# Two-layer hybrid decoder step on one core: expert residual kept by token, last norm on rows, and three small moves in the mixers

## The reference, cut to what matters

```
h = layer_norm(x)
for i in range(2):
    z = h @ w_in[i]                                   # columns of four token mixers
    a_conv = causal_depthwise_conv(past_a, glu(z_a), conv_a_w[i])           # 31 taps, 256 channels
    y_a = silu(layer_norm(a_conv + conv_a_b[i]))
    ...                                               # gated chunk mixer, short conv, pooling
    h = layer_norm(ALPHA * h + concat(y_a, y_b, y_c, y_d) @ w_out[i])
    f = dense_swiglu(h) if i == 0 else moe_swiglu(h)  # top 2 of 8 experts, gates from a softmax
    h = layer_norm(ALPHA * h + f)
```

## Time and profile before

| what | value |
|---|---|
| runs (three) | 1518.63, 1525.19, 1525.61 us; median 1525.19 |
| the profiled execution's own time | 1527.83 us |
| its span, first to last instruction | 1526.1 us |
| mean granted PE clock | 0.992 |
| busy: PE, DVE, ACT, POOL | 1491.5, 1233.2, 962.4, 91.3 us |
| mixer of layer 0; of layer 1 | about 25 to 115 us; 405 to 503 us |
| dense feed-forward | about 117 to 400 us |
| expert stage, from its first cut | about 532 to 1502 us |
| scatter of the last item and last norm | 1502 to 1526 us |

### The profile page before, as it was taken

The page is one execution under the profiler, slowest core; times in us unless marked ns, Lnnn a source line. Parts: engine busy times, 40 slices in busy tenths (PEclk is TensorE's granted clock), DMA queues, the critical chain, the costliest instruction groups (busy, mean ns, idle before and its releaser), DMA issues.

```text
span 1526.1 us, 20555 instructions
## 1 busy us (share of the span) xinstructions
PE 1491.5 (98%) x7963; PEld 1291.2 (85%) x7963; DVE 1233.2 (81%) x1267; ACT 962.4 (63%) x902; POOL 91.3 (6%) x102
## 2 busy tenths in 40 slices
PE   9999999999998999999999999999999998999997
PEld 8969999999996788888888888888888886878886
DVE  7978555544796698899998988898889897989884
ACT  5645433344564477777777777777777776767773
POOL 3402000000020000001000001000000101100000
PEclk9999999999999999999999999999999999999999
DMA  9725544444250389999999999999999999998980
GB/s 342 156 83 197 177 163 164 166 166 166 88 151 20 146 337 389 376 387 391 405 372 369 376 383 372 404 376 367 379 380 383 399 369 347 364 356 339 370 311 31
DMA packets 68154, 439.43 MB, mean 288 GB/s; under 512 B 9504, under 2 KB 13536, under 8 KB 16608
## 3 DMA queue, kind: packets, MB, share of 16 engines
q1 hardware_dynamic: 60320, 424.68, 73.5%
q0 software_dynamic: 4816, 12.32, 2.7%
q10 hardware_dynamic: 2928, 1.18, 0.3%
HBM read 431.06 MB, written 7.09 MB: 287 GB/s over the span
## 4 chain that ended last, share of the span: by engine, by line
PE 75%; issue 15%; DVE 5%; DMA 3%; ACT 2%; POOL 1%; SPq 0%; ACTq 0%; POOLq 0%; DVEq 0%
PE bank L876 45%; PE bank L550 21%; PE bank L684 2%; PE bank L931 1%; DMA ring<-in_w_e_gate 1%; DVE work L1544 1%; DVE w_lo L1950 1%; PE bank L574 1%; DMA x_rows<-token_rows,token_row 1%; PE bank L529 1%; DVE w_lo L1333 1%; PE bank L496 1%; DMA token_rows<-y_rows 1%; PE bank L512 1%; ACT w_hi L1060 1%
## 5 line engine op out<-in xcount | busy, mean ns | idle before, releaser
L1950 DVE TENSOR_TENSOR w_lo<-ring,w_hi 128x2048 fp32r<-128x2048 f32 x320 | 731.4, 2290 | 96.1 <-ACT w_hi L1261 93.7
L1261 ACT ACTIVATE w_hi<-ring 128x2048 fp32r<-128x2048 f32 x320 | 612.9, 1917 | 162.3 <-PE bank L876 162.2
L876 PE MATMUL bank<-w_hi,x_hi 128*128 128x512 f32 x896 | 353.9, 395 | 0.7 <-DVE w_lo L1950 0.6
L876 PE MATMUL bank<-w_hi,x_lo 128*128 128x512 f32 x896 | 349.3, 390 | 0.0
L876 PE MATMUL bank<-w_lo,x_hi 128*128 128x512 f32 x896 | 348.6, 389 | 0.0
L550 PE MATMUL bank<-x_hi,w_hi 128*128 128x290 f32 x664 | 199.3, 300 | 0.6 <-DVE w_lo L1333 0.5
L876 PEld LDWEIGHTS bank<-w_hi,x_lo 128*128 128x128 f32 x896 | 168.2, 188 | 35.8
L876 PEld LDWEIGHTS bank<-w_hi,x_hi 128*128 128x128 f32 x896 | 168.3, 188 | 35.3 <-DVE w_lo L1950 1.2
L550 PE MATMUL bank<-x_lo,w_hi 128*128 128x290 f32 x664 | 197.6, 298 | 0.0
L550 PE MATMUL bank<-x_hi,w_lo 128*128 128x290 f32 x664 | 197.1, 297 | 0.0
L876 PEld LDWEIGHTS bank<-w_lo,x_hi 128*128 128x128 f32 x896 | 168.4, 188 | 33.3
(11 more groups left out here) (296 smaller groups left out, 1777.1 us busy)
## 6 DMA issues: line engine op xcount, KB each, us to landing
ring<-in_w_e_gate SPq DMA_DIRECT2D x112, 1024.0 KB, 7.1
ring<-in_w_e_up SPq DMA_DIRECT2D x112, 1024.0 KB, 7.3
ring<-in_w_e_down SPq DMA_DIRECT2D x112, 1024.0 KB, 7.4
ring<-in_w_in SPq DMA_DIRECT2D x16, 1024.0 KB, 5.8
ring<-in_w_ff_gate SPq DMA_DIRECT2D x14, 1024.0 KB, 5.2
ring<-in_w_ff_up SPq DMA_DIRECT2D x14, 1024.0 KB, 4.9
ring<-in_w_ff_down SPq DMA_DIRECT2D x14, 1024.0 KB, 4.9
ring<-in_w_out SPq DMA_DIRECT2D x8, 1024.0 KB, 9.7
```

Of the source, the lines that this page charges most:

```text
L876: ins = mm(out, x, w[slot][:, columns], start=(first and n == 0), stop=(last and n == 2), skip_group_check=True)
L1261: A(w_hi[(CUT0 + p) % SPLIT][:, :], ring[(START + p) % SLOTS][:, :], ACT.Copy).then_inc(hi_done, 1)
L1950: V.tensor_tensor(w_lo[(CUT0 + p) % SPLIT][:, :], ring[(START + p) % SLOTS][:, :], w_hi[(CUT0 + p) % SPLIT][:, :].bitcast(F32), ALU.subtra ...
```

## The change

Mixers: (1) ACT makes `sample_prods(16, TAPS_A)` before the two cuts `c1` and `c1 + 1`; (2) the bias rides on tap 0's product on ACT, so that DVE's two additions go; (3) PE runs `keep_warm(7, 20)` ahead of the first sums of norm "a".

Expert stage: (4) the residual is `r_tok`, by token (three tiles of 128 x 1024), started as ALPHA times the input rows, and started only when they stand in `x_rows`; POOL waits for that before it overwrites `x_rows`; (5) `scale_first`, `turn_mix` and `add_mix` are gone; `mix(n)` adds one gathered row times its gate straight to `r_tok`, six DVE operations after chunks 13, 15, 18, 21, 29, 31; (6) the last item's scatter gives rows (tokens by 512 values, six outputs), and DVE adds each with an operation that also sums over the row; (7) the last norm is taken on rows, tile by tile, and then turned by PE and stored by the same four DMAs. Unused waits on `x_lo_done` and the bank reuse `added` go.

```diff
-        SCATTER_BANKS = [6, 7, 1, 4, 5, 2, 3, 6]
+        SCATTER_BANKS = [6, 7, 1, 4, 5, 2]
+        SCATTERED = [(0, 0), (1, 0), (0, 1), (1, 1), (2, 0), (2, 1)]
-        SCALE_AT = [8, 14, 26]
-        MIX_AT = [11, 18, 29]
-        ADD_AT = [17, 21, 27, 33, 39, 41]
-        TURN_AT = [("up", 2), ("gate", 3), ("gate", 4), ("gate", 5), ("gate", 6), ("up", 6)]
+        MIX_AT = [13, 15, 18, 21, 29, 31]
...
@@ PE, mixer
                     if n == 4:
+                        keep_warm(7, 20)
                         next(ln_a)
...
@@ PE, last item
-                for d in range(KB):
...
-                        mm(out, y_hi[q][:, d, :], scat[q][:, :], start=(q == of[0]), stop=False)
-                        last = mm(out, y_lo[q][:, d, :], scat[q][:, :], start=False, stop=(q == of[-1]))
+                for n, (t, half) in enumerate(SCATTERED):
...
+                    out = bank[SCATTER_BANKS[n]][0:rows, :]
+                    for q in range(2):
+                        to = scat[q][:, t * P:t * P + rows]
+                        mm(out, to, y_hi[q][:, 4 * half:4 * half + 4, :], start=(q == 0), stop=False)
+                        last = mm(out, to, y_lo[q][:, 4 * half:4 * half + 4, :], start=False, stop=(q == 1))
                     last.then_inc(scattered, 1)
...
@@ PE, end
-            for _ in ln_sums("ffn1", r, sq_l, lambda b: pe.wait_ge(added, n_items * KB + b + 1)):
-                pass
+            keep_warm(0, 20)
+            for t in range(TT):
+                rows = TILE_ROWS[t]
+                pe.wait_ge(tok_normed, t + 1)
+                for k in range(KB):
+                    last = nc.tensor.transpose(bank[k][:, t * P:t * P + rows], r_tok[0:rows, t, k * P:(k + 1) * P],
+                                               ident[0:rows, 0:rows])
+                    if t == TT - 1:
+                        last.then_inc(y_turned, 1)
...
@@ ACT, sample_prods
+                            if tap == 0:
+                                ins = A(out, src, ACT.Identity, scale=w, bias=v_at("conv_a_b", layer, b))
+                            else:
+                                ins = A(out, src, ACT.Copy, scale=w)
...
@@ ACT, mixer
                 first_taps_c()
+                sample_prods(16, TAPS_A)
                 if layer == 0:
                     act.wait_ge(z_ready, 16)
                     bias_parts(vec_at("ln_mix_b", 0))
                 cut(c1)
                 cut(c1 + 1)
-                sample_prods(16, TAPS_A)
...
@@ ACT, item
-                        if after == "hold" and not tabled and p in SCALE_AT:
-                            scale_first(SCALE_AT.index(p))
...
@@ ACT, end
-            large_ln("ffn1", r, vec_at("ln_ffn_g", 1), vec_at("ln_ffn_b", 1))
+            for t in range(TT):
+                rows = TILE_ROWS[t]
+                act.wait_ge(less_mean_done, n_items * TT + t + 1)
+                A(ring[t][0:rows, 0:D_MODEL], r_tok[0:rows, t, :], ACT.Square, bias=less_mean[0:rows, t:t + 1],
+                  accum_out=sq_sum[0:rows, t:t + 1]).then_inc(tok_sq, 1)
+            for b in range(0, KB, 2):
+                act.wait_ge(y_turned, b + 1)
+                A(h[:, b, :], bank[b][:, 0:TOKENS], ACT.Identity, scale=v_at("ln_ffn_g", 1, b),
+                  bias=v_at("ln_ffn_b", 1, b)).then_inc(y_even, 1)
...
@@ DVE, sample_sums
-                    for b in range(MB):
-                        dve.wait_ge(summed_s, 2 * MB * layer + b + 1)
-                        V.tensor_scalar(sample_cols(acc_a[:, b, :]), sample_cols(acc_a[:, b, :]),
-                                        v_at("conv_a_b", layer, b), None, ALU.add).then_inc(summed_s, 1)
...
@@ DVE, extra_items
-                for d in range(KB):
-                    V.tensor_scalar(r[:, d, :], h[:, d, :], ALPHA, None, ALU.mult).then_inc(r_start, 1)
+                def start_rows(t):
+                    dve.wait_ge(rows_staged, t + 1)
+                    V.tensor_scalar(r_tok[:, t, :], x_rows[:, t % 2, :], ALPHA, None, ALU.mult).then_inc(r_start, 1)
...
@@ DVE
-            def mix(t):
+            def mix(n):
+                t, c = n // 2, n % 2
...
-                dve.wait_ge(mix_scaled, t + 1)
-                V.scalar_tensor_tensor(out=first[0:rows, :], in0=second[0:rows, :], scalar=col[0:rows, 5, t:t + 1],
-                                       in1=first[0:rows, :], op0=ALU.mult, op1=ALU.add).then_inc(rows_mixed, 1)
+                V.scalar_tensor_tensor(out=r_tok[0:rows, t, :], in0=mix_rows[t][c][0:rows, :],
+                                       scalar=col[0:rows, 4 + c, t:t + 1], in1=r_tok[0:rows, t, :], op0=ALU.mult,
+                                       op1=ALU.add).then_inc(rows_mixed, 1)
-            def add_mix(n):
...
@@ DVE, last item
-                for d in range(KB):
-                    dve.wait_ge(scattered, n_scat * KB + d + 1)
-                    V.tensor_tensor(r[:, d, :], r[:, d, :], bank[SCATTER_BANKS[d]][:, 0:TOKENS],
-                                    ALU.add).then_inc(added, 1)
+                for n, (t, half) in enumerate(SCATTERED):
...
+                    V.memset(carrier[:, n:n + 1], 0.0)
+                    row_half = r_tok[0:rows, t, 512 * half:512 * half + 512]
+                    V.tensor_tensor_reduce(out=row_half, in0=bank[SCATTER_BANKS[n]][0:rows, :], in1=row_half, scale=1.0,
+                                           scalar=0.0, op0=ALU.add, op1=ALU.add,
+                                           accum_out=row_sum[0:rows, 2 * t + half:2 * t + half + 1]).then_inc(added, 1)
+                    if half:
...
+                        V.tensor_tensor_reduce(out=halves[0:rows, t, :], in0=row_sum[0:rows, 2 * t:2 * t + 2],
+                                               in1=minus_half[0:rows, 0:2], scale=2.0 / D_MODEL, scalar=0.0, op0=ALU.mult,
+                                               op1=ALU.add, accum_out=less_mean[0:rows, t:t + 1]).then_inc(less_mean_done, 1)
...
@@ DVE, end
+            for t in range(TT):
+                rows = TILE_ROWS[t]
+                dve.wait_ge(tok_sq, t + 1)
+                V.tensor_scalar(var_tok[0:rows, t:t + 1], sq_sum[0:rows, t:t + 1], 1.0 / D_MODEL, LN_EPS, ALU.mult,
+                                ALU.add).then_inc(tok_var, 1)
+                dve.wait_ge(tok_rstd, t + 1)
+                V.tensor_scalar(r_tok[0:rows, t, :], r_tok[0:rows, t, :], less_mean[0:rows, t:t + 1],
+                                rstd_tok[0:rows, t:t + 1], ALU.add, ALU.mult).then_inc(tok_normed, 1)
+            for b in range(1, KB, 2):
+                dve.wait_ge(y_turned, b + 1)
+                V.tensor_scalar(h[:, b, :], bank[b][:, 0:TOKENS], v_at("ln_ffn_g", 1, b), v_at("ln_ffn_b", 1, b),
+                                ALU.mult, ALU.add).then_inc(y_odd, 1)
...
@@ POOL
+                        if i == 1:
+                            pool.wait_ge(r_start, TT)
...
                         if t == 2:
-                            pool.wait_ge(mix_turned, 2)
+                            pool.wait_ge(rows_mixed, 2)
...
+            for t in range(TT):
+                rows = TILE_ROWS[t]
+                pool.wait_ge(tok_var, t + 1)
+                G.tensor_tensor(rstd_tok[0:rows, t:t + 1], var_tok[0:rows, t:t + 1], minus_half[0:rows, t:t + 1],
+                                ALU.pow).then_inc(tok_rstd, 1)
```

More of the change, by code:

```diff
@@ L520, in ln_sums @@
                 yield
-                if name == "ffn1":
-                    keep_warm(1, 4)
                 if MEAN_BANK[name] == 7:
@@ L531, in ln_sums @@
                 yield
-                if name == "ffn1":
-                    keep_warm(1, 7)
                 pe.wait_ge(ln_rs, n + 1)
@@ L894, in _ @@
                 pe.sem_inc(s, 2 * TABLED)
-            def turn_mix(n):
-                t, half = n // 2, n % 2
-                rows = TILE_ROWS[t]
-                pe.wait_ge(rows_mixed, t + 1)
-                if n:
-                    pe.wait_ge(mix_added, n)
-                for k in range(4):
-                    kk = 4 * half + k
-                    last = nc.tensor.transpose(bank[7][:, k * P:k * P + rows], mix_rows[t][0][0:rows, kk * P:(kk + 1) * P],
-                                               ident[0:rows, 0:rows])
-                last.then_inc(mix_turned, 1)
             def item(i, e, x_from, after, x_next=None, tabled=False):
@@ L965, in item @@
                         number_rows(x_next)
-                    if after == "hold" and not tabled and ("gate", g) in TURN_AT:
-                        turn_mix(TURN_AT.index(("gate", g)))
                     turn(g - 1)
                     hidden("up", g)
-                    if after == "hold" and not tabled and ("up", g) in TURN_AT:
-                        turn_mix(TURN_AT.index(("up", g)))
                     down(g - 1, 0)
@@ L1230, in _ @@
                 act.wait_ge(s, 64 * DEPTH)
-            def scale_first(t):
-                rows = TILE_ROWS[t]
-                first = mix_rows[t][0]
-                act.wait_ge(mix_rows_in[t], 32)
```

(9 more changed lines are left out.)

87 lines of the change are left out of this document (46 added, 41 removed).

## The result

The changed kernel took 1502.19 us (median of 4 runs, 1501.92 to 1503.56); the kernel before, beside it, 1523.03 us (4 runs, 1518.63 to 1525.61). The ratio is 0.9856 with a 95% interval of 0.9834 to 0.9879. Forecast were 1501.1 us and a range of 1493 to 1510.

What follows compares the result with a forecast made beforehand. PE was taken to bound the expert stage, so only work or waits taken off PE pay. Terms 0 - 4.8 - 14.1 - 5.2 = -24.1 us from 1527.8 give 1503.7, less 2.6 for the median 1501.1; range 1493 to 1510.

Steps and rivals of the forecast that it cites:

- Mixer 1: Norm "a" of mixer 1: earlier products, bias edit and ones start the squares' sums at 478.8, against 483.59; -4.8 us.
- Mixer 0: Norm "a" of mixer 0: ones end 1.6 us after the sums' old start, full clock makes up for it; 0.
- The bounds: Both mixers: if the ones did not hold the clock up, mixer 1 wins only 2.2 us and mixer 0 loses 1.7.
- Item 6: Item 6 of the expert stage: two waits and six turns go, less 0.9 us of short PE waits; -14.1 us.
- The two waits: Item 6: waits behind `scale_first(0)` and at `turn_mix(5)` go with their clock losses, 8.4 and 3.7 us.
- The turns: Item 6: six turns, each putting 0.36 to 0.43 us between matmuls, go; 2.5 us.
- DVE as the bound: Rival, item 6: four mixes in nine cuts make PE wait and lose clock, 3.7 us at two places, 1508; chance 0.13.
- Loads that give the stall back: Rival, item 6: busy DMA queues turn the stall into waits on loads; half 1507, all 1510; chance 0.12.
- The end: From the scatter on: scatter in rows, norm tile by tile, last blocks shared by ACT and DVE; -5.2 us.
- The stores behind it are the same: The end: the stores after ACT's last block were taken as unchanged.
- The exit of the loop: The end: if the loop's exit also costs 1.3 us, the end wins only 2.5 us, its low end.
- Normalising 128 x 1024: The end: not in the trace, priced at 0.8 us; 0.59 by the skill's page, with 0.6 us more won.

Runs made afterwards that it cites:

- run 1: The changed kernel without the 20 ones products ahead of the sums of norm "a" in the mixers; 1499.65 us, ratio 0.9829.
- run 4: The kernel before with three places in item 6 moved (first scaling, first mix, fifth addition), its turns and scales kept; 1515.98 us, ratio 0.9921.
- run 6: The kernel before with the mixers' three edits alone (products ahead of the cuts, bias in ACT's first tap, ones products); 1521.70 us, ratio 0.9976.
- run 11: The kernel before with only the products of taps 16 to 30 moved ahead of the two cuts; 1519.66 us (one run).
- run 12: As run 9, with the six mixes of item 6 after chunks 13, 17, 19, 23, 29, 31; 1499.93 us, ratio 0.9828.
- run 10: The changed kernel again, unaltered, on the chip of runs 9, 11 and 12; 1501.97 us, ratio 0.9847.
- run 9: The changed kernel with the edits of runs 1 and 7 together; 1499.53 us, ratio 0.9835.
- run 3: The changed kernel with the products of taps 16 to 30 behind the two cuts again; 1506.37 us, ratio 0.9861.
- run 8: The changed kernel without the 20 ones products behind the scatter at the end; 1502.36 us (one run).
- run 7: The changed kernel with the last norm's variances ahead of the previous tile's normalising and 20 of the end's 40 ones records; 1500.61 us, ratio 0.9839.

## Why the prediction came out right, point by point

- **Mixer 1, forecast -4.8, measured -5.4.** The steps held: the sums start behind the ones at 474.04 (474.8 forecast), then 3.9 us to the squares' sums (4.0). The ones' 4.63 us are the forecast 4.7; PE ended its block 0.5 us earlier. That the cuts cost nothing held: one waits for its chunk as before, and DVE comes to them much later.
- **Mixer 0, forecast 0, measured -0.3.** The trade of ones against clock came out even, as worked out. The bounds ("if the ones did not hold the clock up, mixer 1 would win only 2.2 and mixer 0 lose 1.7") took for granted that without the ones the clock would be down after 3 us. This is a step whose reason fell, beside that of the stores below: in that state it is down in some executions and up in others, and run 1 was faster without the ones.
- **Item 6, forecast -14.1, measured -14.5.** The two waits were priced with their clock losses at 8.4 + 3.7 + 0.4 = 12.5 us; run 4 took 12.2 away by places alone. The turns less PE's new waits were 2.5 - 0.9 = 1.6 in the forecast and 2.3 by subtraction. PE's new short waits came to 0.8 us as two pieces of 0.48 and 0.33, against 0.9 forecast. That the forecast agrees this well is partly luck: the stall of 6.08 us was one execution's, and in runs 6 and 11 it was 3.5 and 2.8 us shorter, the expert stage 4.1 and 3.2 us.
- **DVE as the bound** got only those 0.8 us; run 12 shows that they came from mixes too close to each other. **Loads that give the stall back**: not seen, ACT has no wait for a ring slot in item 6 and the expert stage kept its length within 0.12 us over seven runs with the same places (1004.32 to 1004.44).
- **The end, forecast -5.2, measured -5.6.** The two agree because two errors cancel. From the scatter's start to the end of ACT's last block it was 21.0 us and is 14.2, where 15.8 were forecast, so that step gave 1.6 us more. "The stores behind it are the same" was wrong by 1.1 us the other way: with ACT and DVE sharing the blocks, the four stores come within 2.02 us in place of 3.48 and keep each other waiting. In detail, the scatter took 5.6 (5.3 forecast), the handovers 1.53 us a tile in place of 2.0, so that ACT ended 8.6 us after the scatter and not 10.5. Mis-sized was the power on POOL: I had taken 0.89 from a row with three values per partition, and with one value it takes 0.57. The exit of the loop, priced at up to 1.3 us, cost nothing that shows.
- **Normalising 128 x 1024** took 0.81 us, where the rows before gave 0.8. The table of the Trainium skill (VectorE: DVE Perf Modes, the section on the TRN2 errata) gives 0.59 as an estimate, and the page itself adds that this row of it under-predicts the time of a single operation; the trace agrees with the remark and not with the table.
- **Sum and median.** The terms gave -24.1 where the spans differ by 25.8; the profiled execution was forecast at 1503.7 us and took 1502.39. From there to the median of the runs the forecast took off 2.6 us, the shift of the kernel before, while the changed kernel's profiled run is its median within 0.2. The two errors go against each other, which is why 1501.1 lies so close to 1502.19. Between medians the change is 20.8 us beside the four runs of the result and 24.3 in run 10's group.

## What to carry to other kernels

A wait for a gather costs what it costs in that execution, so before moving work into other layouts, move the waiting operation behind the latest landing seen: here three numbers brought 12.2 of 14.5 us between the profiled executions and 9.8 us by the medians. When work at the end of a kernel gets faster, price the stores behind it at their own pace: here they took back 1.1 us. Ones products that bridge a pause of TensorE should end just before the work they wait for; beyond that every record is paid in full. When runs of a variant spread, sort them by their granted clock before comparing medians.

## What the runs showed of the hardware that I had not expected

- After pauses of 2.7 to 3.1 us TensorE went on at 2.4 GHz or at 1.2 GHz with no relation to the length of the pause: 3.09 us kept it and 3.01 us lost it in one execution, and 2.72 us ahead of mixer 1's sums kept it in run 1 and lost it in runs 9 and 12. Full-rate products right ahead of the pause did not help in the one case seen (run 3: 4.6 us of ones, 2.70 us of pause, then half clock).
- The clock can fall after the pause: in run 12, mixer 1, some 0.6 us after PE had resumed from 2.72 us, with PE at work; in run 8 1.1 us after it had resumed from 2.84 us, as it stood again for 0.45 us.
- The stall for the same indirect gather was 6.08, 2.6 and 3.3 us in three executions of the same code in item 6, and 2.2 to 2.5 us of that spread is the wait for the table's last store ahead of it.
- Four stores of 288 KB issued within 3.48 us landed 2.2 us after their issue; issued within 2.02 us they took 2.3 to 3.1 us, at 371 to 388 GB/s.
- GpSimd's power took 0.54 to 0.57 us for one value per partition and 0.89 for three, so three single ones (2.34 us with their gaps in run 7) cost over twice one of three.
